# Two of the four weight sums of each Strassen pair move from VectorE to accumulating transfers that GpSimd issues

## What is computed

```python
def rms_norm(x, gain):
    xf = x.astype(jnp.float32)
    y = xf * lax.rsqrt(jnp.mean(xf * xf, axis=-1, keepdims=True) + RMS_EPS)
    return (y * gain.astype(jnp.float32)).astype(x.dtype)

def swiglu(x, w_gate, w_up, w_down):
    return (jax.nn.silu(x @ w_gate) * (x @ w_up)) @ w_down
```

## Time and profile before

| What | Value |
|---|---|
| median of 3 runs | 1973.09 us (1972.71 to 1973.41) |
| profiled execution, its own time | 1972.95 us |
| its span | 1971.2 us |
| TensorE (PE) busy | 1948.4 us, 99% |
| TensorE weight load (PEld) busy | 1706.2 us, 87% |
| VectorE (DVE) busy | 1473.0 us, 75% |
| ScalarE (ACT) busy | 856.1 us, 43% |
| GpSimd (POOL) busy | 448.2 us, 23% |
| transfers | 189.35 MB, mean 96 GB/s |
| chain that ended last | PE 85%, DVE 8%, ACT 3%, issue 2%, DMA 1%, POOL 1% |

### The profile page before, as it was taken

The page is one execution under the profiler, slowest core; times in us unless marked ns, Lnnn a source line. Parts: engine busy times, 40 slices in busy tenths (PEclk is TensorE's granted clock), DMA queues, the critical chain, the costliest instruction groups (busy, mean ns, idle before and its releaser), DMA issues.

```text
span 1971.2 us, 28646 instructions
## 1 busy us (share of the span) xinstructions
PE 1948.4 (99%) x11710; PEld 1706.2 (87%) x11710; DVE 1473.0 (75%) x1948; ACT 856.1 (43%) x1229; POOL 448.2 (23%) x324
## 2 busy tenths in 40 slices
PE   7999999999999999999999999999999999999999
PEld 6899998877789999988999998877777888999997
DVE  7888886555598888878888886773458568988884
ACT  6434433535554333345443344442546344433432
POOL 1322122142331112222211222200015412222111
PEclk9999999999999999999999999999999999999999
DMA  4333232351132332233333323222200233333333
GB/s 160 107 98 106 97 106 80 127 181 55 58 103 97 107 107 98 97 93 104 104 97 108 101 92 113 96 93 89 75 1 1 86 96 102 112 97 103 101 88 105
DMA packets 68482, 189.35 MB, mean 96 GB/s; under 512 B 6528, under 2 KB 14976, under 8 KB 68352
## 3 DMA queue, kind: packets, MB, share of 16 engines
q1 hardware_dynamic: 68352, 187.52, 29.5%
HBM read 182.78 MB, written 4.72 MB: 95 GB/s over the span
## 4 chain that ended last, share of the span: by engine, by line
PE 85%; DVE 8%; ACT 3%; issue 2%; DMA 1%; POOL 1%; SPq 0%; DVEq 0%; ACTq 0%
PE BANKS L600 11%; PE BANKS L602 11%; PE BANKS L601 11%; PE BANKS L535 9%; PE BANKS L536 9%; PE BANKS L537 9%; PE BANKS L650 6%; PE BANKS L651 5%; PE BANKS L652 5%; PE BANKS L956 2%; DVE LO L1551 1%; DMA RING<-gu_dram 1%; PE BANKS L933 1%; DVE ASR L1560 1%; PE BANKS L784 1%
## 5 line engine op out<-in xcount | busy, mean ns | idle before, releaser
L2129 POOL TENSOR_TENSOR TMP<-TMP,RSTD 128x512 f32<-128x512 f32 x88 | 136.0, 1546 | 840.0 <-ACT TMP L1102 840.0
L535 PE MATMUL BANKS<-XH,HI 128*128 128x512 f32 x624 | 246.8, 395 | 11.7 <-DVE XL L1497 11.2
L600 PE MATMUL BANKS<-BF,ASH 128*128 128x256 f32 x876 | 248.5, 284 | 2.4 <-ACT MID L1120 1.4
L601 PE MATMUL BANKS<-BFL,ASH 128*128 128x256 f32 x876 | 247.9, 283 | 0.0
L602 PE MATMUL BANKS<-BF,ASL 128*128 128x256 f32 x876 | 247.9, 283 | 0.0
L536 PE MATMUL BANKS<-XL,HI 128*128 128x512 f32 x624 | 244.2, 391 | 0.0
L537 PE MATMUL BANKS<-XH,LO 128*128 128x512 f32 x624 | 243.7, 391 | 0.0
L1551 DVE TENSOR_TENSOR LO<-RING,HI 128x1024 fp32r<-128x1024 f32 (+2 forms) x204 | 218.1, 1069 | 25.1 <-ACT HI L1092 24.8
L1102 ACT ACTIVATE TMP<-TMP 128x512 f32<-128x512 f32 x88 | 55.6, 632 | 390.1 <-DVE TMP L1588 390.0
L650 PE MATMUL BANKS<-HH,DHI 128*128 128x512 f32 x496 | 194.1, 391 | 1.8 <-DVE DLO L1638 1.8
L651 PE MATMUL BANKS<-HL,DHI 128*128 128x512 f32 x496 | 193.8, 391 | 0.0
(11 more groups left out here) (244 smaller groups left out, 4789.4 us busy)
## 6 DMA issues: line engine op xcount, KB each, us to landing
RING<-gu_dram SPq DMA_DIRECT2D x176, 512.0 KB, 3.4
DRAW<-down_dram SPq DMA_DIRECT2D x48, 512.0 KB, 3.6
RING<-oin_dram SPq DMA_DIRECT2D x32, 512.0 KB, 3.4
RING<-down_dram SPq DMA_DIRECT2D x32, 384.0 KB, 3.2
RING<-ein_dram SPq DMA_DIRECT2D x16, 512.0 KB, 3.5
RING<-oout_dram SPq DMA_DIRECT2D x16, 512.0 KB, 3.4
DRAW<-down_dram SPq DMA_DIRECT2D x16, 384.0 KB, 3.4
RING<-eout_dram SPq DMA_DIRECT2D x8, 512.0 KB, 3.6
```

The costliest lines, as they stand in the source:

```text
L535: pe.matmul(PS[bank][:], HI[j][:, c], hi(k), start=(n == 0), stop=False)
L600: pe.matmul(out, w_hi[:, c], x_hi(k), start=(k == 0), stop=False)
L601: pe.matmul(out, w_hi[:, c], x_lo(k), start=False, stop=False)
```

## The change

The instruction `sums_first` of VectorE goes, and with it one of three increments of `sum_made` for each pair. In its place, for each of the 73 Strassen pairs:

- SyncE loads sums 0 and 1 with their first operand: two transfers of 128 x 512 floats (256 KB each), the left half of the up unit into `ASR[:, b, 0]` and the right half of the gate unit into `ASR[:, b, 1]`, straight from the weights in HBM. For the first two pairs of a feed-forward block they stand behind the loads of units 5 and 7; for the later ones ahead of the load of the pair's up unit, behind a wait for `seven_done` of pair p-2, which was the last to read that buffer.
- GpSimd waits for both (`pair_in`) and issues one transfer of 128 x 2 x 512 floats that adds the left half of the gate unit, read again from HBM, onto both (`add_pair`). For the first two pairs of a block it stands between the GpSimd instructions of plain pairs 0 and 1; for the later ones it stands at the head of iteration p-2 of GpSimd's loop.
- `sums_second` now waits for that transfer (`pair_sum`) and for the slot `RAW[2b]`, and no longer for both slots of the pair. ScalarE's first `sums_split` waits for the same transfer.
- In pairs with an early piece VectorE's list goes from first, second, mid_two, third, mid_five to mid_two, second, mid_five, third.

```diff
+                def load_pair(p):
+                    b = p % 2
+                    if p >= PLAIN[f] + 2:
+                        sp.wait_ge(seven_done, block_count(f, p - 2) + 1)
+                    sp.dma_start(ASR[:, b, 0, :], gu_d[f, 2 * p + 1, :, 0:4 * P]).then_inc(pair_in[b], 16)
+                    sp.dma_start(ASR[:, b, 1, :], gu_d[f, 2 * p, :, 4 * P:8 * P]).then_inc(pair_in[b], 16)
+
                 plain = 2 * PLAIN[f]
                 for n in range(SLOTS, NU):
                     u = n if n < plain else n ^ 1
+                    if n % 2 == 0 and n // 2 >= PLAIN[f] + 2:
+                        load_pair(n // 2)
                     load(q0 + n // 4, n % 4, gu_d[f, u])
+                    if n in (5, 7):
+                        load_pair(PLAIN[f] + (n == 7))
...
-                def sums_first(p):
-                    b, q = p % 2, (base + 2 * p) // 4
-                    dve.wait_ge(weights_in[2 * b], 16 * (q + 1))
-                    dve.wait_ge(weights_in[2 * b + 1], 16 * (q + 1))
-                    gate = RAW[2 * b + 1]
-                    other = PAIR[b][:].rearrange("p (t c) -> p t c", c=4 * P)[:, 0:6:5, :]
-                    dve.tensor_tensor(ASR[:, b, 0:2, :], other, gate[:, 0:4 * P].unsqueeze(1).to_broadcast([P, 2, 4 * P]),
-                                      ALU.add).then_inc(sum_made, 1)
-
-                def sums_second(p):
-                    b, g = p % 2, block_count(f, p)
-                    dve.wait_ge(sum_made, 3 * g + 1)
+                def sums_second(p):
+                    b, q = p % 2, (base + 2 * p) // 4
+                    dve.wait_ge(weights_in[2 * b], 16 * (q + 1))
+                    dve.wait_ge(pair_sum[b], 16 * pair_count(f, p))
                     dve.tensor_tensor(ASR[:, b, 2, :], ASR[:, b, 1, :], RAW[2 * b][:, 0:4 * P],
                                       ALU.add).then_inc(sum_made, 1)
...
             def block_ffn(f, r):
+                def add_pair(p):
+                    b = p % 2
+                    gate_left = gu_d[f, 2 * p, :, 0:4 * P].unsqueeze(1).to_broadcast([P, 2, 4 * P])
+                    pool.wait_ge(pair_in[b], 32 * pair_count(f, p))
+                    pool.dma_start(ASR[:, b, 0:2, :], gate_left, accum_op=ALU.add).then_inc(pair_sum[b], 16)
+
                 for p in range(FT):
+                    if PLAIN[f] <= p < FT - 2:
+                        add_pair(p + 2)
                     pool.wait_ge(silu_ready, 22 * f + p + 1)
                     pool.tensor_tensor(GT[:, p % 2, :], GT[:, p % 2, :], RSTD[:], ALU.mult).then_inc(sr_ready, 1)
+                    if p < 2:
+                        add_pair(PLAIN[f] + p)
                     pool.wait_ge(hh_ready, 22 * f + p + 1)
```

More of the change, by code:

```diff
@@ L318, in trunk @@
         sum_made, sum_hi, sum_lo = sem("sum_made"), sem("sum_hi"), sem("sum_lo")
+        pair_in, pair_sum = ([sem(f"{n}{b}") for b in range(2)] for n in ("pair_in", "pair_sum"))
         late_in = [sem(f"late_in{s}") for s in range(SLOTS)]
@@ L361, in block_count, with pair_count @@
             return sum(FT - PLAIN[i] for i in range(f)) + p - PLAIN[f]
+        def pair_count(f, p):
+            same = [(i, n) for i in range(f + 1) for n in range(PLAIN[i], FT) if n % 2 == p % 2]
+            return same.index((f, p)) + 1
         def early_count(f, p):
@@ L1095, in sums_split @@
                     g = block_count(f, p)
-                    act.wait_ge(sum_made, 3 * g + (3 if i else 1))
+                    if i:
+                        act.wait_ge(sum_made, 2 * g + 2)
+                    else:
+                        act.wait_ge(pair_sum[p % 2], 16 * pair_count(f, p))
                     act.activation(ASH[:, p % 2, 2 * i:2 * i + 2, :], ASR[:, p % 2, 2 * i:2 * i + 2, :],
@@ L1570, in sums_third @@
                     b, g = p % 2, block_count(f, p)
-                    dve.wait_ge(sum_made, 3 * g + 2)
+                    dve.wait_ge(sum_made, 2 * g + 1)
                     dve.tensor_tensor(ASR[:, b, 3, :], ASR[:, b, 2, :], RAW[2 * b][:, 4 * P:8 * P],
@@ L1672, in block_ffn @@
                     split(9, whole)
-                    sums_first(first)
                     up(3)
@@ L1711, in block_ffn @@
                 sums_third(first)
-                dve.wait_ge(sum_made, 3 * block_count(f, first) + 3)
+                dve.wait_ge(sum_made, 2 * block_count(f, first) + 2)
                 gate(first - 1)
@@ L1721, in block_ffn @@
                     if has_early(f, p):
-                        sums_first(nxt)
+                        mid_two(p)
                         sums_second(nxt)
-                        mid_two(p)
+                        mid_five(p)
                         sums_third(nxt)
-                        mid_five(p)
                         if leads(f, p):
                             early_split(p)
-                        dve.wait_ge(sum_made, 3 * block_count(f, nxt) + 3)
+                        dve.wait_ge(sum_made, 2 * block_count(f, nxt) + 2)
                         split(2 * nxt, whole)
```

1 line of the change is left out of this document (removed).

## The result

The changed kernel takes 1977.53 us in the median of 11 runs (1974.19 to 1980.3), against 1972.71 (1971.58 to 1973.43) for the kernel before in as many: a ratio of 1.0025, 95% interval 1.0017 to 1.0033. It is slower by 4.8 us, 0.25%. The forecast was 1971.0, a little faster; the range (1966.8 to 1981) holds the measured time, the direction was wrong.

The account below looks back on a forecast made before the run. TensorE, busy 99% of the span, sets the time. Against the profiled 1972.95 us, stalls gone -4.91 and late first pairs +2.8 give 1970.85, as median 1971.0 us; range 1966.8 to 1981.

Parts of the forecast that it names:

- What goes: Stalls in Strassen pairs that vanish with VectorE's 73 instructions: 4.91 us of 6.4 us, at f = 0 to 3.
- SyncE's queue and GpSimd's issue: SyncE's queue is not held up; a GpSimd issue up to about 7 us costs TensorE nothing.
- Transfer engines: In the steady stretch, 1 MB more per pair takes them from 0.34 to under 0.6.
- Where the transfer has to be in time: Allowed T: 6.1 us at first pairs of f = 2 and 3, 8.1 at their pair 17, 12 elsewhere.
- T may be 12 us: At every other pair an early piece of over 4 us lies between as well, giving this allowance.
- T: Time from GpSimd's issue to the sum's landing: taken as 7.5 us at the first pair, 6.6 elsewhere.
- signs of being wrong: `sums_second` waiting in steady pairs, `TMP` over 3 us behind a block's end, or matmuls slower beside more transfers.
- Lateness goes on one to one: First pairs of f = 2 and 3: each sum 1.4 us late, passed on to TensorE, cost 2.8 us.
- is worth nothing in the sum: VectorE-GpSimd exclusion: up to 0.4 us more per pair comes free on both engines, hidden under TensorE's cover.
- not late at 6.6: Pair 17 of f = 2 and 3: sum lands at 1114.3 + T, needed by 1122.4, so T may be 8.1 us.
- The median stands 0.14 above the profiled execution: The median of the runs is 0.14 above the profiled one, so 1970.85 us becomes 1971.0.
- the transfer is slow: Rival: T over 9.3 us makes first pairs and pair 17 late; 1979.8 us at T = 10; chance 0.20.

Follow-up runs that it names:

- e4: Changed kernel without GpSimd's transfer, VectorE waiting for SyncE's halves alone (two sums lack the gate's left half): 1966.16 us, ratio 0.9967.
- e8: The changed kernel once more, nothing edited, for a second profile: 1978.6 us, 3.1 above the first profile.
- e10: Changed kernel with first pair's sum issued ahead of first multiply, second's behind HL(1), pair 17 of f = 2 and 3 summed by VectorE: 1967.12 us.
- e9: Changed kernel with each block's second Strassen pair's sum issued by GpSimd behind HL(1) instead of ahead of it: 1973.73 us, ratio 1.0007.
- e11: Changed kernel with pair 17 of f = 2 and 3 summed by VectorE again, nothing else: 1975.51 us, ratio 1.0015.
- e6: Changed kernel with GpSimd's issue of each block's first Strassen pair's sum moved later, behind HL(0): 1978.58 us in 8 runs.

## Why the prediction was wrong

By its own steps:

- **What goes: right.** f = 0 and f = 1 show no wait; the `DLO` of 0.76 in f = 3 is gone. e4 puts all of VectorE's part at 6.5 us, the 6.4 of the earlier trace rows.
- **SyncE's queue and GpSimd's issue: right.** The issue takes 1.20 us, far from the 7 us from which it would have cost.
- **Transfer engines: somewhat too low.** They reach 0.65 where I said under 0.6. No matmul is slower for it, but SyncE's 512 KB take 4.5 us instead of 3.4.
- **Where the transfer has to be in time: right places, but "T may be 12 us" elsewhere was too generous.** First pair 6.1 us holds, and pair 17's 8.1 within 0.2 (its terms, 1110.8 + 0.8 + 2.9, give 1114.5 and so 7.9). In pairs 5 and 8 VectorE already waits at 8.9, which was one of my signs of being wrong, and TensorE's `DLO` comes 0.39 us late at T = 9.6 (e8) and 0.50 late at 9.8 (e10): by these two the limit is about 9.2, an estimate. In the profiled execution it cost nothing.
- **T: mis-sized.** "I take T = 7.5 at the first pair and 6.6 elsewhere." Measured: 8.43 and 8.18 at the first pairs (issue 909.91, last packet at 918.34; 1644.00 and 1652.18), 8.2 in the median. The landing was therefore 2.3 and 2.1 us late, not 1.4. This is 1.6 us of the error.
- **"Lateness goes on one to one", and contention "is worth nothing in the sum": the step that failed.** A sum that lands late does not only shift VectorE's list, it moves it onto GpSimd's `HL(1)`, which the change had itself delayed, and the stall then stands at `LO` and `ASL`, not at `MID` as I wrote. In f = 2: landing 2.3 late, second sum 2.35 instead of 0.68 (+1.7), `LO` 1.22 instead of 1.60 (-0.4), sum 3.6; the excess grew by 4.82 - 1.18 = 3.64. In f = 3: 2.1, and `LO` 2.38 instead of 1.60 (+0.8), sum 2.9; it grew by 3.41 - 0.49 = 2.92. Forecast 2 x 1.4 = 2.8, measured 6.6. "SBUF — State Buffer" in the Trainium skill, section on who interferes with whom, says that a VectorE instruction with two SBUF inputs contends with a GpSimd one that reads SBUF, and that this is an exclusive lock; the trace agrees (0.69 against 2.35 us). I had looked it up for the instruction that goes, where it could only win. I did not ask where the shifted list would meet GpSimd. e9 removes just this meeting: the second sum is back at 0.69 us with the landing as late as before, and the first pairs' excess falls by 2.6 us.
- **Pair 17: "not late at 6.6": wrong by two terms.** SyncE issued the halves where I had them (1112.43, and 1110.8 plus the 1.64 us by which the program then was late). The second took 4.5 us to land and not the 2.9 of the median, so GpSimd issued at 1117.56 and not at 1115.9, and the sum took 7.36 us instead of 6.6. It landed at 1124.92 where 1122.4 plus 1.64 was the limit: 0.9 late, and the wait is 0.94. In the second profile it is 2.17. e11 prices the place at 2.0 us.
- **The median stands 0.14 above the profiled execution: not so for the changed kernel.** There it stands 2.0 above. By their mean clocks (0.998 in seven of eleven) most executions seem to have matmuls at the lower clock behind the stall of f = 2, as e8's profile shows them; the profile of before could not, having no stall of 3 us in a Strassen pair. The clock is not all of it: the seven are 3.1 us longer in the mean than the other four, e8's lower clock costs 1.25, and the run at the median itself has a clock of 1.0.

The sum by these terms, against the profiled execution: f = 0 and 1 -2.03, first pairs +6.56, pairs 16 and 17 and the `DLO` waits -2.02 (3.20 to 1.18), together +2.5; the spans differ by 2.6. From there to the median's +4.8 the one longer execution that was profiled (e8) has most of its extra time at the lower clock of f = 2 and at pair 17; that the others do too is inferred from their clocks and from e11. The error of 6.5 us is then 1.6 for T, 2.1 for contention, 1.2 at pair 17 and 1.9 between the profiled execution and the median, less 0.3 by which f = 0 and f = 1 won more than I had said.

Of the rivals, "the transfer is slow" was the nearer one: its place was right, its point of decision (T = 9.3) was too high: with the landing at 8.2 to 8.4 the profiled execution was already 2.6 us slower, because a late microsecond cost more than one.

What stays open: why transfers of the same place take 0.7 us more in one execution than in another (pair 17's 7.4 and 8.1, pair 5's 8.9 and 9.6), and what decides whether the clock falls after a stall of 3.1 us. The runs show both happen; none of them varied one of these by itself.

## What to carry to other kernels

When an instruction is replaced by a transfer, look for the one place where the transfer is *issued* late, not where it runs: here 4 of 73 decided most of it, and moving two issues on GpSimd's queue, with two sums given back to VectorE, turned 0.25% slower into 0.28% faster. Price lateness along the shifted list: what runs on the other engine in the microseconds into which it moves. And a queued issue that waits for data holds everything behind it; put it behind the work that is ready.

## What the runs showed of the hardware

- A 512 KB accumulating transfer issued by GpSimd took 5.8 to 9.7 us to land, 8.2 in the median, and its issue 1.20 us of GpSimd; the same without adding 6.9 us and 0.74; SyncE's plain 512 KB took 3.4 us before and 4.5 beside them. "DMA: Bandwidth & Descriptors" in the Trainium skill, section on the anatomy of one DMA on the GpSimd path, has about 2.0 us plus the bytes over 436 GB/s, by which 512 KB are 3.2 us, an estimate. The measurement decides: no transfer of GpSimd here was as quick, the shortest plain one 4.4 us.
- Accumulating nearly doubled the packets (19856 against 10512 for the same 38.28 MB, so 1.9 KB each against 3.6 in the mean). From the shares of 16 engines' span a packet took 0.175 us in the mean (0.110 x 16 x 1973.8 / 19856), and 0.195 us without adding (0.065 x 16 x 1965.7 / 10512).
- VectorE's 128x512 addition takes 0.69 us, and 2.35 us beside a GpSimd instruction of 1.75 us: 1.66 us longer, nearly the whole of that one. Beside GpSimd's issue of a transfer alone it keeps its 0.69 us (changed kernel, f = 3, at 1653.00, the issue at 1653.09).
- TensorE's granted clock fell to 0.50 within an idle time of 3.15 us and stood there for 6.8 us (e8), and at the end of one of 3.69 us and stood there for 3.4 (e11); it stayed at 1.00 after 3.07 us in the first profile of the changed kernel and 3.11 in e6's.
